# The third block's long convolution placed behind its recurrence, and every high part of a weight made by a product on GpSimd

## The reference, cut to what matters

```
proj = u @ w_in
x_lru, g_lru, v_cc, g_cc = split(proj, 512 columns each)
xc = causal_depthwise_conv(x_lru, 4 taps) + b
y_lru = rg_lru(xc) * gelu(g_lru)          # h_t = a_t h_{t-1} + sqrt(1 - a_t^2) (i_t x_t)
c = v_cc * sigmoid(g_cc)
c = causal_depthwise_conv(c, 31 taps) + b
y_cc = silu(layernorm(c))
y = concatenate([rmsnorm(y_lru), rmsnorm(y_cc)])
h = h + y @ w_out
```

## Time and profile before

| | us |
|---|---|
| median of 3 runs | 3770.02 (3769.31 to 3771.95) |
| the profiled execution | 3772.37 |
| its span, first to last instruction | 3770.5 |
| TensorE busy | 3387.6 (90%) |
| DVE busy | 1335.9 (35%) |
| GpSimd busy | 1236.1 (33%) |
| ACT busy | 732.4 (19%) |

### The profile page before, as it was taken

The page is one execution under the profiler, slowest core; times in us unless marked ns, Lnnn a source line. Parts: engine busy times, 40 slices in busy tenths (PEclk is TensorE's granted clock), DMA queues, the critical chain, the costliest instruction groups (busy, mean ns, idle before and its releaser), DMA issues.

```text
span 3770.5 us, 37623 instructions
## 1 busy us (share of the span) xinstructions
PE 3387.6 (90%) x15562; PEld 2718.2 (72%) x15562; DVE 1335.9 (35%) x1667; ACT 732.4 (19%) x1078; POOL 1236.1 (33%) x1052
## 2 busy tenths in 40 slices
PE   5967976899959899999999999994888989999997
PEld 4546855778848578787888888883875678888886
DVE  4154055133150540312441111116898463222223
ACT  2220054121020540101210000003333321000101
POOL 3201300435414024243453443441442344344331
PEclk9968998999979899999999999996989999999998
DMA  3100100102121001112111111112002011111111
GB/s 117 45 17 28 45 1 14 65 33 91 45 95 45 12 23 56 45 45 90 45 55 46 45 46 54 44 45 73 34 23 78 28 40 52 48 44 46 54 44 45
DMA packets 31635, 179.48 MB, mean 48 GB/s; under 512 B 3744, under 2 KB 4768, under 8 KB 14624
## 3 DMA queue, kind: packets, MB, share of 16 engines
q1 hardware_dynamic: 18864, 137.37, 10.6%
q10 hardware_dynamic: 12656, 40.42, 2.9%
HBM read 163.10 MB, written 14.68 MB: 47 GB/s over the span
## 4 chain that ended last, share of the span: by engine, by line
PE 81%; DVE 13%; ACT 3%; issue 2%; POOL 1%; DMA 0%; DVEq 0%; ACTq 0%; POOLq 0%
PE ps L420 46%; PE ps L451 16%; PE ps L477 5%; PE ps L1752 2%; DVE c_out L2176 2%; PE ps L1851 1%; PE ps L1394 1%; PE ps L734 1%; PE ps L1410 1%; DVE n_sq L355 1%; ACT p L901 1%; DVE xlo L361 1%; PE ps L308 1%; DVE n_acc L287 1%; PE ps L300 1%
## 5 line engine op out<-in xcount | busy, mean ns | idle before, releaser
L517 POOL TENSOR_TENSOR whi<-raw,par 128x512 fp32r<-128x512 f32 x131 | 147.7, 1127 | 2428.5 <-PE ps L420 1749.4
L521 POOL TENSOR_TENSOR wlo<-raw,whi 128x512 fp32r<-128x512 f32 x524 | 796.0, 1519 | 41.7
L420 PE MATMUL ps<-xhi,whi 128*128 128x512 f32 x2304 | 720.1, 394 | 44.0 <-DVE xlo L361 16.1
L420 PE MATMUL ps<-xlo,whi 128*128 128x512 f32 x2304 | 714.1, 391 | 0.0
L420 PE MATMUL ps<-xhi,wlo 128*128 128x512 f32 x2304 | 713.3, 391 | 0.0
L420 PEld LDWEIGHTS ps<-xhi,whi 128*128 128x128 f32 x2304 | 433.8, 189 | 146.7 <-issue 23.7
L420 PEld LDWEIGHTS ps<-xlo,whi 128*128 128x128 f32 x2304 | 435.8, 189 | 91.7
L420 PEld LDWEIGHTS ps<-xhi,wlo 128*128 128x128 f32 x2304 | 435.1, 189 | 91.7
L519 POOL CAST whi<-raw 128x512 fp32r<-128x512 f32 x393 | 314.0, 799 | 0.0
L451 PE MATMUL ps<-hidden_lo,whi 128*128 128x512 f32 x864 | 269.1, 393 | 0.0
L451 PE MATMUL ps<-hidden_hi,whi 128*128 128x512 f32 x864 | 268.3, 392 | 0.4 <-DVE hidden_lo L1274 0.4
(11 more groups left out here) (435 smaller groups left out, 4057.3 us busy)
## 6 DMA issues: line engine op xcount, KB each, us to landing
raw<-stream SPq DMA_DIRECT2D x131, 1024.0 KB, 4.8
h_scr<-h ACTq DMA_DIRECT2D x2, 4096.0 KB, 12.2
x_in<-xT ACTq DMA_DIRECT2D x4, 1024.0 KB, 14.4
x_again<-xT ACTq DMA_DIRECT2D x4, 1024.0 KB, 8.1
h<-h_scr ACTq DMA_DIRECT2D x1, 4096.0 KB, 13.0
outT<-h ACTq DMA_DIRECT2D x8, 512.0 KB, 3.1
bias<-bias ACTq DMA_DIRECT2D x1, 2560.0 KB, 18.5
o_scr<-o_staged ACTq DMA_DIRECT2D x2, 1024.0 KB, 4.8
```

What stands on the lines that cost most here:

```text
L420: mm = nc.tensor.matmul(ps[:, c0 + c:c0 + c + width], w, x(k, a, width), start=(n == 0 and m == 0), stop=(n == len(ks) - 1 and m == 2))
L517: nc.gpsimd.tensor_tensor(WHI[:, r, t], RAW[:, r, t], one, ALU.mult).then_inc(hi_done, 1)
L521: ins = nc.gpsimd.tensor_tensor(WLO[:, r, t], RAW[:, r, t], WHI[:, r, t].bitcast(F32), ALU.subtract)
```

## The change

```diff
                 for piece in range(PIECES_W):
                     t = slice(TILES // PIECES_W * piece, TILES // PIECES_W * (piece + 1))
-                    if piece == 0:
-                        one = par("ones", 0, P).unsqueeze(1).to_broadcast([P, TILES // PIECES_W, P])
-                        nc.gpsimd.tensor_tensor(WHI[:, r, t], RAW[:, r, t], one, ALU.mult).then_inc(hi_done, 1)
-                    else:
-                        nc.gpsimd.tensor_copy(WHI[:, r, t], RAW[:, r, t]).then_inc(hi_done, 1)
+                    one = par("ones", 0, P).unsqueeze(1).to_broadcast([P, TILES // PIECES_W, P])
+                    nc.gpsimd.tensor_tensor(WHI[:, r, t], RAW[:, r, t], one, ALU.mult).then_inc(hi_done, 1)
...
-            for o in range(3):
-                lru_half(o)
-            cc_sums(3)
-            lru_half(3, (2, cc_columns))
-            lru_half(4, (1, cc_spreads))
-            for o in range(5, 8):
-                lru_half(o)
+            for o in range(2):
+                lru_half(o)
+            cc_sums(2)
+            for o in range(2, 6):
+                lru_half(o)
+            cc_sums(3)
+            lru_half(6, (2, cc_columns))
+            lru_half(7, (1, cc_spreads))
...
             keep_v(2)
-            short_first(2)
             keep_g(2)
-            long_first(2)
             rates(2)
             rate_square(2)
-            keep_v(3)
             rate_root(2)
             short_first(3)
+            keep_v(3)
+            long_first(2)
             keep_g(3)
-            long_first(3)
-            keep_l(0)
             rates(3)
             rate_square(3)
+            keep_l(0)
+            rate_root(3)
+            long_first(3)
             keep_l(1)
-            rate_root(3)
             keep_l(2)
-            keep_l(3)
...
             short_convolution(2)
-            taps(1, 17, CCK)
-            gate_input(2)
-            taps(2, 1, 5)
+            taps(1, 6, 18)
             recurrence(2, 0)
-            taps(2, 5, 8)
+            taps(1, 18, 21)
             recurrence(2, 1)
-            taps(2, 8, 13)
+            taps(1, 21, 23)
             recurrence(2, 2)
             short_convolution(3)
-            taps(2, 13, 15)
+            gate_input(2)
+            taps(1, 23, CCK)
+            taps(2, 1, 3)
             gate_input(3)
-            taps(2, 15, 24)
             recurrence(3, 0)
...
-            taps(3, 22, CCK)
+            taps(2, 25, CCK)
+            taps(3, 1, CCK)
```

More of the change, by code:

```diff
@@ L1820, in spread @@
                 return mm
-            for b in range(4):
-                row_sums(b, OTHER, b)
+            for b in range(3):
+                row_sums(LRU_SUM[b], OTHER, b)
             cc_sums(0)
-            cc_sums(1)
+            row_sums(LRU_SUM[3], OTHER, 3)
             pe.wait_ge(*L("l_root", 1))
             columns(0, OTHER).then_inc(S("l_cols"), 1)
-            cc_sums(2)
+            cc_sums(1)
             pe.wait_ge(*L("l_diag", 1))
-            spread(DIAG3, OTHER).then_inc(S("l_inv"), 1)
+            spread(INVC, OTHER).then_inc(S("l_inv"), 1)
             slot = WH["out_3a"][0]
@@ L2031, in act_block3, with square_lru @@
             act.dma_start(HL3[0][:, :, :], h_blocks[:, 0:4, :]).then_inc(S("h3_loaded0"), 16)
-            act.wait_ge(S("cc_conv"), 3 * (CCK - 1))
-            for b in range(4):
+            act.wait_ge(S("cc_conv"), 2 * (CCK - 1))
+            def square_lru(b):
                 act.wait_ge(S("y_lru_done"), b + 1)
-                square(b, YLW[:, b, META:LW])
-            act.wait_ge(*L("m_sum", 4))
+                square(LRU_SUM[b], YLW[:, b, META:LW])
+            square_lru(0)
+            square_lru(1)
+            keep_l(3)
+            square_lru(2)
+            square(CC_SUM[0], CCO[:, 0, :])
+            square_lru(3)
+            act.wait_ge(*L("m_sum", LRU_SUM[3] + 1))
             nc.scalar.activation(ROWS3[0:1, :], ps[0:1, OTHER:OTHER + T], ACT.Sqrt, bias=EPSC[0:1, :], scale=1.0 / (4 * P))\
                 .then_inc(S("l_root"), 1)
-            for b in range(3):
-                square(4 + b, CCO[:, b, :])
+            square(CC_SUM[1], CCO[:, 1, :])
             for b in range(4):
@@ L2050, in keep_half @@
                 nc.scalar.activation(HL3[o // 4][:, o % 4, :], ps[:, c0:c0 + T], ACT.Copy).then_inc(S("lh_kept"), 1)
-            for o in range(2):
+            keep_half(0)
+            act.wait_ge(S("cc_conv"), 3 * (CCK - 1))
+            square(CC_SUM[2], CCO[:, 2, :])
+            for o in range(1, 5):
                 keep_half(o)
             act.wait_ge(S("cc_conv"), 4 * (CCK - 1))
-            square(7, CCO[:, 3, :])
-            keep_half(2)
+            square(CC_SUM[3], CCO[:, 3, :])
+            keep_half(5)
             act.wait_ge(*L("m_sum", 8))
-            for row in (32, 0):
-                nc.scalar.activation(ROWS3[row:row + 1, :], ps[row:row + 1, OTHER + 2 * BANK:OTHER + 2 * BANK + T], ACT.Copy)\
-                    .then_inc(S("cc_rows"), 1)
+            nc.scalar.activation(ROWS3[0:33, :], ps[0:33, OTHER + 2 * BANK:OTHER + 2 * BANK + T], ACT.Copy).then_inc(S("cc_rows"), 1)
             act.wait_ge(*L("cc_var", 4))
             nc.scalar.activation(RCOL[:, :], VCOL[:, :], ACT.Sqrt, bias=EPSC).then_inc(S("cc_root"), 1)
-            keep_half(3)
-            keep_half(4)
+            keep_half(6)
             for b in range(4):
@@ L2184, in dve_block3, with gate_lru @@
             gate_input(0)
[L2185 removed]
+            taps(0, 1, 8)
             short_convolution(0)
[L2187 removed]
+            taps(0, 8, 15)
             recurrence(0, 0)
[L2189 removed]
+            taps(0, 15, 18)
             recurrence(0, 1)
[L2191 removed]
+            taps(0, 18, 20)
             recurrence(0, 2)
             short_convolution(1)
+            taps(0, 20, 26)
+            gate_input(1)
             taps(0, 26, CCK)
[L2195 to L2196 removed]
             recurrence(1, 0)
[L2198 removed]
+            taps(1, 1, 4)
             recurrence(1, 1)
[L2200 removed]
+            taps(1, 4, 6)
             recurrence(1, 2)
             short_convolution(2)
[L2203 to L2205 removed]
+            taps(1, 6, 18)
             recurrence(2, 0)
[L2207 removed]
+            taps(1, 18, 21)
             recurrence(2, 1)
[L2209 removed]
+            taps(1, 21, 23)
             recurrence(2, 2)
             short_convolution(3)
[L2212 removed]
+            gate_input(2)
+            taps(1, 23, CCK)
+            taps(2, 1, 3)
             gate_input(3)
[L2214 removed]
             recurrence(3, 0)
[L2216 removed]
+            taps(2, 3, 6)
             recurrence(3, 1)
[L2218 removed]
+            taps(2, 6, 8)
             recurrence(3, 2)
[L2220 to L2222 removed]
+            def gate_lru(b):
                 kept("l", b)
@@ L2225, in dve_block3 @@
                 nc.vector.tensor_tensor(y, y, GL[:, b, :], ALU.mult).then_inc(S("y_lru_done"), 1)
-            taps(3, 10, 18)
+            taps(2, 8, 11)
+            dve.wait_ge(S("l_scan"), 4)
+            gate_lru(0)
+            gate_lru(1)
+            taps(2, 11, 16)
+            gate_lru(2)
+            taps(2, 16, 19)
+            gate_lru(3)
+            taps(2, 19, 23)
             dve.wait_ge(*L("l_cols", 1))
@@ L2229, in dve_block3 @@
             v.wait()
-            spread_column(DIAG3, LCOL).then_inc(S("l_diag"), 1)
-            taps(3, 18, 22)
+            spread_column(INVC, LCOL).then_inc(S("l_diag"), 1)
+            taps(2, 23, 25)
             dve.wait_ge(*L("l_inv", 1))
```

31 lines of the change are left out of this document (10 added, 21 removed).

## The result

The changed kernel takes 3781.87 us in the median of 8 runs (3777.67 to 3785.09), the kernel before 3769.66 (3767.42 to 3772.93) on the same chips: ratio 1.003, 95% interval 1.0019 to 1.0041. The forecast was 3781, slower, by 12.0 us of products outside the mixing stage and -1.1 for the stage itself. The profile of the changed kernel has a span of 3780.5 us, 10.0 more than before.

What follows compares the result with a forecast made beforehand. The chain was mostly TensorE, but the third block's mixing stage was bound by DVE's queue. Profiled 3772.4 us + 12.0 (products outside the stage) - 1.1 (stage) = 3783.3, so 3781 for the median; range 3766 to 3794.

Steps and rivals of the forecast that it cites:

- Part 1: GpSimd's weight splits: three of four casts a slot become products, costing 12.0 us outside the mixing stage, bounds 9 and 15.
- Memory attention: Short slots there: three TensorE waits for splits, each longer by three products at 0.48 us, 4.3 us in all.
- Norms and the rest: Products replace casts ahead of DVE operations on the chain outside the mixing stage; 7.7 us including the start.
- The product's price: On GpSimd and in DVE's delay, a product costs 0.48 us more than the cast it replaces.
- Part 2: New order in the third block's mixing stage, with products' cost there included: gives 1.1 us, bounds -14 and +12.
- Idle: DVE's pauses in the mixing stage, first to last tap: 6.9 us instead of 14.1, bounds 4 and 12.
- Products in the stage: In nine splits of the mixing stage, 27 products for casts at 0.48 us delay DVE by 13.0 us.
- Disturbance apart from products: Mixing stage: GpSimd delays DVE by 35.5 us as before, plus 5.0 for one more split among the taps.
- Rival 3: Mixing stage's last tap later still, at 2937.7, as splits hit DVE fully; stage costs 9 us: 3791, chance 0.16.
- Tail: Last tap to end of the convolution half's first output column: 41.2 us instead of 53.1, half clock included.
- Rival 1: Order gains 14 us in the mixing stage, where products cost DVE little more than casts: 3768, chance 0.22.
- Rival 2: DVE absorbs the products' longer hold everywhere; only memory attention's 4.3 us and the order's 14 count: 3760, chance 0.12.

Runs made afterwards that it cites:

- e3: Changed order, with four products a slot only in slots 88 to 97 and one product with three casts elsewhere; 0.5 us faster than the kernel before, ratio 0.9996.
- e9: Changed order, four products in every slot except 88 to 97, which keep one product and three casts; 0.7 us faster than the kernel before, ratio 0.9998.
- e1: The changed kernel with the old split of one product and three casts, so the new order alone; 15.3 us faster than the kernel before, ratio 0.9961.
- e2: The kernel before with a product for every piece, its order unchanged; 21.3 us slower than the kernel before, ratio 1.006.
- e5: e1 with three output halves ahead of the last convolution sums instead of six; 3.3 us faster than the kernel before, ratio 0.9989.
- e4: e1 with each low part's subtraction replaced by a cast of the raw weights (wrong numbers); 45.9 us faster than the kernel before, ratio 0.9878.
- e6: e1 with each slot split in eight pieces instead of four; 18.4 us faster than the kernel before, ratio 0.9947.
- e10: e8 with eight pieces a slot and four more taps ahead of each of recurrences 1, 2 and 3; 3735.18 us, ratio 0.9911 to the kernel before.
- e7: e1 with each slot split in two pieces instead of four; 11.0 us slower than the kernel before, ratio 1.0026.
- e8: e1 with each slot's product cut to 16 columns and the rest of that piece cast; 23.7 us faster than the kernel before, ratio 0.9939.

## Why the prediction was right, and where two of its terms were not

That the forecast of 3781 lies within 1 us of the measured median is in part luck: each run's place is known to some us only, and in the stage two misses of 5.2 and 4.4 us cancel. What the runs bear out is the way it is made up: the products' price by operation, paid in and outside the stage, against an order whose gain lies in the tail.

**Part 1, outside the stage: 12.0 forecast, or 10.6 without the three products of slot 88. The runs, which leave that slot out, say 12.7 and 14.6 (changed less e3; e9 less e1), so at least 2 us more, within some 5 either way.** Its places:
- Start: 3 casts, 1.4 us. The last squares of the first norm start at 30.25 instead of 28.80: right.
- Memory attention: 4.3 was too small. The waits are 4.28, 2.07 and 4.52 us, of which the middle one was put at 2.9. But counting waits was the wrong step: the splits are a chain of their own there, and TensorE's first matmul behind them moved from 687.62 to 693.01, by 5.4, of which 0.1 had been there at 647.7. That is 5.3 us, 11 products at 0.48. Two casts of the first slot are on that chain too, though no wait shows them. And TensorE needs 1.0 us more for the 192 matmuls behind them (46.4 against 45.4), at a granted clock of 0.92 in the mean and not 0.94, so that it is 6.3 by the first softmax (e2 lost 6.0 there, e9 5.5). The chain before and after:

```profile
740.56 1.24 DVE soft_c L1152
```

```profile
688.09 1.04 POOL whi L516
...
746.90 1.24 DVE soft_c L1149
```

- Norms and the rest: at the first tap the shift is 8.6 us (2656.40 to 2664.99) where the terms up to there, 1.4 + 4.3 + 4.3, give 10. Since the memory attention alone took 2 more, about 3.5 are missing. At 350 us the changed kernel runs 2.5 us ahead of before, and TensorE's granted clock from 130 to 340 us is 0.82 in place of 0.78. The edit is not what raised it: e1, e3 and e5, which up to there are the kernel before, have 0.83, 0.82 and 0.81, and are 3.3 to 4.1 us ahead at 640 us. The one trace of before was slow in this stretch, and a shift against it is sure to some 4 us only. Behind the stage the norm adds 2.4, for 4 products at 0.48.
- Full slots: TensorE busy 130 of 130 us, no wait: right.
- The product's price: 0.48 us beside GpSimd's 1092 and 612 ns. Of GpSimd's 208 us, some 190 are products; the subtractions, whose work is the same, are 16 longer. The trace's price held against the 0.63 us estimated from the Trainium skill's figures (GPSIMD Engine Reference, section 2.1 for the 2.5 cycles, 3.1 for the 1.03). The times alone could not have told them apart: the 12.7 and 14.6 are sure to some 5 us, and the estimate gave 15.7.

**Part 2, the stage: -1.1 forecast, -1.5 in the trace** (the end of the first column moved by 7.1 us, the first tap by 8.6). The runs say -0.5 for e3, which is the stage and slot 88's three products (1.4). But it is the sum of two misses that cancel.
- Idle: 6.9 forecast, 6.3 measured. The last scan ends at 2843.15 (2844 forecast). TensorE's wait of 14.5 us for the gates of recurrence 2 is gone, and the last tap came no earlier for it: right.
- Products in the stage: 13.0 forecast. e1 and the changed kernel, both less their idle time, differ by 12.4: right.
- **Disturbance apart from products: the failed term.** Forecast 35.5 + 5.0 for one more split, 40.5; e1 has 264.3 - 4.3 - 214.3 = 45.7. One more split is eight operations. But of before's 62 GpSimd operations from first to last tap 7 lay for the most part in DVE's idle time, of e1's 70 none. So e1's taps and recurrences meet 8 more subtractions, 5 more casts and 2 more products: 8 x 0.91 + 5 x 0.23 + 2 x 0.71 = 9.9, against 10.2 measured. Idle time taken from DVE was free time for GpSimd. Rival 3 named this ("DVE pauses less than before, so splits hit it fully") and had 2937.7 for the last tap; in the same frame (less the 8.6 us of the first tap) it ended at 2935.1, nearer to rival 3 than to the forecast's 2931.1.
- **Tail: mis-sized the other way.** 41.2 forecast, 36.8 measured; at full clock the sum was 34.2. TensorE waited 15.1 us, not the 9 forecast, and the clock fell to half, as said (0.54 from 2933 to 2948), but only the sums at the wait's end paid, 3.30 us in place of the 1.81 that the same eight took in before:

```profile
2923.95 1.81 PE ps L1803 x8
```

Behind them the clock is 1.00 for 7 us and 0.96 over 42. The columns and quarters had been priced at half clock too. The last low parts took 1.82 each beside a split, as allowed for.
- What the tail's gain is made of was read right in the sum ("six of eight output halves are done by then") and is shown by e5. The first part's sentence that the stage is DVE's queue end to end was wrong for its last 60 us: from 2906 us on the chain of before was TensorE's.

**The rivals.** Rival 1 had the right value of the order (14 us; e1 has 15.3), by the same two misses, and was wrong about the products: e3 is 14.8 above e1. Rival 2, an absorbed hold, falls with the taps of 2.01 us. Of the markers, two of the three waits, GpSimd's busy time (208 us more, about 190 forecast) and the taps' mean (1654 ns, forecast above 1.6) came as said.

## What to carry to other kernels

An edit that lengthens another engine's operations must be priced together with the edit that fills the waiting engine's pauses: the fuller a queue, the more of a neighbour's port time it meets. Price a collision by operation (its length less a constant), and ask on both sides: small pieces spare the one engine and hold up the other, which waits about once for each. When an engine's operations become shorter, move its fillers with them, or the gain turns into a wait for whoever was next (e4, e6), and it is there to be had by reordering (e10). Where an end is bound by another queue than the fullest one, or the fullest one still has pauses, part of any loss is hidden, and a reordering that removes this cover makes the loss count in full.

## What the runs showed of the hardware

- A tap of 1.30 us beside GpSimd is longer by the duration of GpSimd's operation less 0.38 to 0.40 us, for nine operations between 0.40 and 2.40 us long and of three kinds (e1, e6, e7). An operation of 0.22 us directly ahead of a cast cost a tap some 0.15 us more than the cast alone (e8).
- The loss goes both ways: a cast of 0.40 us takes 1.39 beside a queue of taps, a product of 1.09 takes 2.07.
- TensorE's granted clock was mostly at the lower of its two levels (1.2 of 2.4 GHz; 0.54 in the mean) over the 15 us that hold the end of its wait and its last sums, and 0.96 over the 42 us behind them: a wait of 15 us cost some 1.5 us by the clock, not the 5.3 that had been allowed.
- The same code is not equally fast up to 640 us in every execution: by 3.3 to 4.1 us in the traces of e1, e3 and e5 against before, with a granted clock of 0.81 to 0.83 against 0.78 from 130 to 340 us.
